# Products of probabilities and values in plain float32 in the two attention loops of a fused 4-layer block

## What is computed

```python
# stick-breaking, 16 heads of 64, query blocks of 128, keys before the query only
z = einsum('bhqd,bhkd->bhqk', q, k) * scale
log_stay = where(strict, log_sigmoid(-z), 0)
w = where(strict, exp(log_sigmoid(z) + reverse_cumsum(log_stay) - log_stay), 0)
out = einsum('bhqk,bhkd->bhqd', w, v)          # <- this product

# dilated: three banded softmax branches, merged by their denominators
p = exp(z - m);  den = sum(p)
o = einsum('brhnqk,brhnkd->brhnqd', p, v) / den   # <- and this one
```

## Time and profile before

| what | value |
|---|---|
| median of 3 runs | 2716.75 us |
| profiled execution, its own time | 2715.01 us |
| span of that execution in the trace | 2713.2 us |
| mean granted TensorE clock | 0.974 |
| TensorE matmul busy | 2593.8 us (96%) |
| VectorE / ScalarE / GpSimd busy | 1474.8 / 903.2 / 217.5 us |
| stick stage: fill and loop / drain | about 40 to 285 us / 285 to 317 us |
| dilated stage: fill and loop / drain | about 741 to 982 us / 982 to 1011 us |

### The profile page before, as it was taken

The page is one execution under the profiler, slowest core; times in us unless marked ns, Lnnn a source line. Parts: engine busy times, 40 slices in busy tenths (PEclk is TensorE's granted clock), DMA queues, the critical chain, the costliest instruction groups (busy, mean ns, idle before and its releaser), DMA issues.

```text
span 2713.2 us, 33021 instructions
## 1 busy us (share of the span) xinstructions
PE 2593.8 (96%) x12138; PEld 2125.8 (78%) x12138; DVE 1474.8 (54%) x2276; ACT 903.2 (33%) x1291; POOL 217.5 (8%) x201
## 2 busy tenths in 40 slices
PE   5999899999899989999999999999999998999998
PEld 4877678888677767888887888778888787788886
DVE  4556464553456655555326555476653466766644
ACT  3334242222334434222223233253331454533311
POOL 0000000000011100000002000000003164000031
PEclk8999799999999979999999999999999999999999
DMA  3111033322211103332222111223322321233332
GB/s 122 52 48 39 31 109 96 97 85 90 88 55 46 54 23 104 100 99 86 90 95 94 62 50 58 86 86 100 93 85 93 132 63 63 86 101 93 92 102 86
DMA packets 60918, 219.49 MB, mean 81 GB/s; under 512 B 6789, under 2 KB 7077, under 8 KB 60720
## 3 DMA queue, kind: packets, MB, share of 16 engines
q1 hardware_dynamic: 58752, 209.53, 24.6%
q0 software_dynamic: 2064, 8.97, 1.0%
q10 hardware_dynamic: 32, 0.02, 0.0%
HBM read 216.38 MB, written 2.12 MB: 81 GB/s over the span
## 4 chain that ended last, share of the span: by engine, by line
PE 84%; DVE 7%; ACT 4%; issue 3%; POOL 1%; DMA 0%; SPq 0%; DVEq 0%; ACTq 0%; POOLq 0%
PE ps L255 27%; PE ps L257 26%; PE ps L256 26%; PE ps L1683 2%; POOL dilated_t L1183 1%; ACT wh L241 1%; DVE wl L249 1%; PE ps L911 1%; DVE stick_left L1060 1%; PE ps L924 1%; ACT window_p L1350 1%; DVE rstd L441 0%; ACT dilated_pB L1002 0%; DVE dilated_pB L1077 0%; PE ps L1707 0%
## 5 line engine op out<-in xcount | busy, mean ns | idle before, releaser
L255 PE MATMUL ps<-xh,wh 128*128 128x512 f32 x2000 | 802.4, 401 | 15.6 <-DVE stick_qs L1172 5.7
L257 PE MATMUL ps<-xh,wl 128*128 128x512 f32 x2000 | 786.0, 393 | 0.0
L256 PE MATMUL ps<-xl,wh 128*128 128x512 f32 x2000 | 785.5, 393 | 0.0
L249 DVE TENSOR_TENSOR wl<-raw,wh 128x1024 fp32r<-128x1024 f32 x332 | 409.6, 1235 | 221.9 <-ACT wh L241 221.6
L241 ACT ACTIVATE wh<-raw 128x1024 fp32r<-128x1024 f32 x332 | 349.1, 1054 | 521.5 <-PE ps L257 504.9
L255 PEld LDWEIGHTS ps<-xh,wh 128*128 128x128 f32 x2000 | 380.8, 190 | 97.3 <-DVE wl L249 8.4
L257 PEld LDWEIGHTS ps<-xh,wl 128*128 128x128 f32 x2000 | 379.5, 190 | 81.8
L256 PEld LDWEIGHTS ps<-xl,wh 128*128 128x128 f32 x2000 | 380.9, 190 | 75.3 <-issue 0.5
L255 PE MATMUL ps<-wh,up_ah 128*128 128x512 f32 x528 | 209.5, 397 | 0.0
L257 PE MATMUL ps<-wh,up_al 128*128 128x512 f32 x528 | 209.3, 396 | 0.0
L256 PE MATMUL ps<-wl,up_ah 128*128 128x512 f32 x528 | 209.3, 396 | 0.0
(11 more groups left out here) (302 smaller groups left out, 3650.5 us busy)
## 6 DMA issues: line engine op xcount, KB each, us to landing
raw<-weights SPq DMA_DIRECT2D x388, 512.0 KB, 3.5
cst<-rows_d POOLq DMA_DIRECT2D x9, 512.0 KB, 5.1
hT<-x_t SPq DMA_DIRECT2D x8, 256.0 KB, 5.8
hgrn_mask<-levels POOLq DMA_DIRECT2D x1, 2048.0 KB, 8.2
window_bias<-bias_rows POOLq DMA_DIRECT2D x1, 2048.0 KB, 10.4
out_t<-hT SPq DMA_DIRECT2D x8, 256.0 KB, 2.2
cst<-consts SPq DMA_DIRECT2D x1, 960.0 KB, 7.9
stick_resets<-resets SPq DMA_DIRECT2D x1, 640.0 KB, 9.6
```

Of the source, the lines that this page charges most:

```text
L249: dve.tensor_tensor(wl[slot][:, :], raw[slot][:, :], wh[slot][:, :].bitcast(F32), ALU.subtract).then_inc(lo_done, 1)
L255: pe.matmul(out, w_hi, m_hi, start=first, stop=False, **kw)
L256: pe.matmul(out, w_hi, m_lo, start=False, stop=False, **kw)
L257: return pe.matmul(out, w_lo, m_hi, start=False, stop=last, **kw)
```

## The change

In both attention stages V and the transposed probabilities are kept as one plain float32 tensor each. `pe_values` issues one plain float32 matmul per block in place of three reduced ones. The low part of the probabilities (`dve_pT`, one VectorE instruction per head) and the low part of V (two per pair) are gone, with their signals; `pe_values` waits for ScalarE's copy alone, and the wait for V's tensor is for ScalarE's two copies. GpSimd clears one padded tensor of V per stage in place of two. What leaves is 16 `ptl` and 16 `vl` instructions per stage.

```diff
-                self.vh, self.vl = a("vh", [P, SB, 2, P], F32R), a("vl", [P, SB, 2, P], F32R)
+                self.v = a("v", [P, SB, 2, P])
-                self.pth, self.ptl = a("pth", [P, self.cols], F32R), a("ptl", [P, self.cols], F32R)
+                self.pt = a("pt", [P, self.cols])
...
         def pe_values(pe, a, j, hh):
-            pe.wait_ge(*a.pl_ready(2 * j + hh + 1))
+            pe.wait_ge(*a.pt_ready(2 * j + hh + 1))
             if hh == 0:
-                pe.wait_ge(*a.v_ready(j + 1))
+                pe.wait_ge(*a.v_ready(2 * j + 2))
             for kb in range(SB):
                 at, n = K_AT[kb], (SB - kb) * P
-                mm = products(pe, ps[:, 6, kb * P:kb * P + n], a.vh[:, kb, hh, :], a.vl[:, kb, hh, :],
-                              a.pth[:, at:at + n], a.ptl[:, at:at + n], hh == 0 and kb == 0,
-                              hh == 1 and kb == SB - 1, skip_group_check=True)
+                mm = pe.matmul(ps[:, 6, kb * P:kb * P + n], a.v[:, kb, hh, :], a.pt[:, at:at + n],
+                               start=hh == 0 and kb == 0, stop=hh == 1 and kb == SB - 1, skip_group_check=True)
             mm.then_inc(a.pv_done.sem, 1)
...
-            act.activation(a.pth[:, :], flat(3, 6)[:, 0:a.cols], ACT.Copy).then_inc(a.ph_ready.sem, 1)
+            act.activation(a.pt[:, :], flat(3, 6)[:, 0:a.cols], ACT.Copy).then_inc(a.pt_ready.sem, 1)
...
-                    act.activation(a.vh[:, :, v, v * HD:(v + 1) * HD], vT, ACT.Copy).then_inc(a.vh_ready.sem, 1)
+                    act.activation(a.v[:, :, v, v * HD:(v + 1) * HD], vT, ACT.Copy).then_inc(a.v_ready.sem, 1)
...
-        def dve_pT(dve, a, j, hh):
-            dve.wait_ge(*a.ph_ready(2 * j + hh + 1))
-            dve.tensor_tensor(a.ptl[:, :], flat(3, 6)[:, 0:a.cols], a.pth[:, :].bitcast(F32),
-                              ALU.subtract).then_inc(a.pl_ready.sem, 1)
...
             if attn:
-                dve_pT(dve, a, j, 0)
                 if a.kind == "stick":
                     dve_weights(dve, a, j, 1)
...
-            if attn:
-                dve_pT(dve, a, j, 1)
...
-            if proj:
-                dve.wait_ge(*a.vh_ready(2 * i + 2))
-                for v in range(2):
...
-                    m = dve.tensor_tensor(a.vl[:, :, v, cols], vT, a.vh[:, :, v, cols].bitcast(F32), ALU.subtract)
-                m.then_inc(a.v_ready.sem, 1)
```

More of the change, by code:

```diff
@@ L866, in __init__ @@
                 self.vs_ready, self.vT_done = Signal("pair_vs_ready", PAIRS), Signal("pair_vT_done", PAIRS)
-                self.vh_ready, self.v_ready = Signal("pair_vh_ready", HEADS), Signal("pair_v_ready", PAIRS)
+                self.v_ready = Signal("pair_v_ready", HEADS)
                 self.z_done, self.p_ready = Signal("pair_z_done", HEADS), Signal("pair_p_ready", HEADS)
-                self.pT_done, self.ph_ready = Signal("pair_pT_done", HEADS), Signal("pair_ph_ready", HEADS)
-                self.pl_ready, self.pv_done = Signal("pair_pl_ready", HEADS), Signal("pair_pv_done", HEADS)
+                self.pT_done, self.pt_ready = Signal("pair_pT_done", HEADS), Signal("pair_pt_ready", HEADS)
+                self.pv_done = Signal("pair_pv_done", HEADS)
                 self.oh_ready, self.o_ready = Signal("pair_oh_ready", PAIRS), Signal("pair_o_ready", PAIRS)
-                self.padded = Signal("pair_padded", 2)
+                self.padded = Signal("pair_padded", 1)
                 if kind == "stick":
@@ L947, in pe_pair @@
                 if attn:
-                    pe.wait_ge(*a.v_ready(i))
+                    pe.wait_ge(*a.v_ready(2 * i))
                 project(pe, ph, i, 0, ps[:, 7 if attn else 0, :], xh, xl, x_ready=x_ready)
@@ L1161, in dve_pair @@
                 dve.tensor_tensor(ol, src, oh.bitcast(F32), ALU.subtract).then_inc(a.o_ready.sem, 1)
-            if proj:
-                dve.wait_ge(*a.vh_ready(2 * i + 2))
-                for v in range(2):
-                    vT = ps[:, 7, :].rearrange("p (b d) -> p b d", b=SB)[:, :, v * HD:(v + 1) * HD]
-                    cols = slice(v * HD, (v + 1) * HD)
-                    m = dve.tensor_tensor(a.vl[:, :, v, cols], vT, a.vh[:, :, v, cols].bitcast(F32), ALU.subtract)
-                m.then_inc(a.v_ready.sem, 1)
         def take(dve, a, dst, bank=7):
@@ L2006, in _ @@
             pool.memset(stick.left[:, TRI:TRI + 1], 0.0).then_inc(ones_made, 1)
-            for v in (stick.vh, stick.vl):
-                pool.memset(v[:, :, :, :].bitcast(F32), 0.0).then_inc(stick.padded.sem, 1)
+            pool.memset(stick.v[:, :, :, :], 0.0).then_inc(stick.padded.sem, 1)
             pool.dma_start(table[0:BUCKETS, :], buckets).then_inc(sinks_in, 16)
             pool.dma_start(one_hot[0:BUCKETS + 1, :], onehot).then_inc(sinks_in, 16)
-            pool.wait_ge(*stick.padded(2))
+            pool.wait_ge(*stick.padded(1))
             pool.memset(table[BUCKETS:BUCKETS + 1, :], NEG).then_inc(sinks_neg, 1)
             pool.wait_ge(*o_up0.tile_done(KT))
-            for v in (dil.vh, dil.vl):
-                pool.memset(v[:, :, :, :].bitcast(F32), 0.0).then_inc(dil.padded.sem, 1)
+            pool.memset(dil.v[:, :, :, :], 0.0).then_inc(dil.padded.sem, 1)
             pool.wait_ge(loaded, 16 * 4)
@@ L2050, in attention_pe @@
                     stats=None if stats_bank is None else lambda: rms_pe(pe, r, stats_bank))
-            pe.wait_ge(*a.padded(2))
+            pe.wait_ge(*a.padded(1))
             with pe.Fori(1, PAIRS) as i:
```

## The result

The changed kernel takes 2686.03 us (median of 4 runs, 2679.3 to 2689.66) against 2716.74 for the kernel before, measured on the same chip. The ratio is 0.9887, with an interval of 0.9875 to 0.9898: 30.7 us less, where 8.7 were forecast. The profiled execution took 2689.66 with a span of 2687.9, against 2715.01 and 2713.2 before, so the traces have 25.3 us to account for. All times and medians here are of executions in the usual state of the chip; one of the four of the kernel `e3_three_no_low` took 4436.95 us at a mean granted clock of 0.66 and is left out.

The account below looks back on a forecast made before the run. TensorE, busy 96% of the span, was taken to bound the kernel. Stick loop +1.8, stick drain -3.5, dilated loop -3.7 and dilated drain -3.3 gave -8.7 us, from 2716.75 to 2708.0, range 2700.5 to 2716.5.

Parts of the forecast that it names:

- Part 1: Products with V: four plain ones take 2.17 us a head at full clock, +0.30; about 4.3 at half clock, +0.7.
- HGRN row: Profile row of HGRN's plain float32 product with V on 1280 columns, 2.20 us, used to price the new products.
- rival B: All 32 product groups: a plain group costs 1.30 times the reduced one, 2.43 us; total 2716.3; chance 0.12.
- Part 2: Stick loop: wait before the second head's turn goes, -4.8, second product +2.1; -2.7 us at unchanged clock.
- The clock: Stick loop: new iteration lengths shift the low-clock spells, from -12.5 to +6.7 us; +1.8 taken, leaning to more spells.
- rival A: Stick loop: the clock stays up, -25 us at most, about 2695; chance 0.10.
- Part 3: Stick drain: waits for the low part go; -1.2 us at low clock, -5.9 if the clock stays up; -3.5 taken.
- Part 4: Dilated loop: projection of v starts earlier, -0.83, second product +0.30; -0.53 us an iteration, -3.7 over seven.
- Part 5: Dilated drain: -1.3 us at low clock, -7 if turn, second product and output projection's start run at full; -3.3 taken.
- The sum: Whole kernel: +1.8 - 3.5 - 3.7 - 3.3 = -8.7 us, giving 2708.0.
- C: Both loops: low clock after every stretch of scores makes it slower, 2727.7 with one in each dilated iteration; chance 0.06.
- D: Both loops: the low part only covered other waits, so only the +0.30 a product remains; 2720; chance 0.06.

Follow-up runs that it names:

- e3_three_no_low: Kernel before with its three reduced products kept but the low part of the probabilities and its wait dropped, output wrong, for timing alone: 2682.28 us, ratio 0.9879.
- fourth kernel: Plain products as in the changed kernel, but VectorE still makes the low part of the probabilities and the product waits for it: 2724.19 us, ratio 1.0031.

## Why the prediction was wrong, point by point

**Part 1, the products: right.** 2.15 us at full clock (2.17 forecast) and 4.43 at half (about 4.3). The HGRN row was the right one to lean on; rival B, at 2.43, is out. By the Trainium skill (FP8 and Floating Point Precision, TensorE Precision Notes) true float32 takes four passes. By that, as an estimate, four times 1280 columns at 2.4 GHz are 2.13 us, and the trace agrees with its 2.15. To apply four against three to the old group (2.49) would have misled: its 1.87 are more than the 1.60 that the same working gives for three passes.

**Part 2, stick loop.** The lengths by kind were right: 30.79, 32.36 and 34.00 against 30.9, 32.4 and 34.1. The wait for the scan's product went, and TensorE is the later one, by 0.7 us (0.66 forecast). At an unchanged clock the forecast was -2.7; the second trace has 30.7 us of low clock in the loop, exactly as the kernel before, and gained 3.3.

**The clock is the step that failed.** In the stick loop the prediction took it for a loss: +1.8 where an unchanged clock gives -2.7, so +4.5 for the clock, on the ground that a spell had stood where the iteration was long. For the output projection with the dilated fill, and for what lies behind the dilated drain, it has no term and gives no reason. The runs showed a gain from the clock, in all three traces of the changed kernel, and not each time in the same places:

| stretch | forecast, us | first trace | second | third |
|---|---|---|---|---|
| start to first transposes | 0 | +1.1 | +1.0 | +0.8 |
| stick loop | +1.8 | -16.0 | -3.3 | -3.4 |
| stick drain | -3.5 | -3.7 | -6.5 | -6.5 |
| output projection to dilated fill | 0 | -4.7 | -5.2 | -5.2 |
| dilated loop | -3.7 | -2.65 | -4.2 | -4.2 |
| dilated drain | -3.3 | -3.8 | -4.9 | -4.9 |
| behind it, to the last matmul | 0 | +4.45 | -2.65 | -2.7 |
| sum | -8.7 | -25.3 | -25.8 | -26.1 |
| low clock (before: 130 us) | | 99 | 92 | 92 |

In the first trace the stick loop lost 27 us of low clock, the mechanism of rival A, with more than the -12.5 that I had for it. (That figure left the first iteration alone; it lost two of its three spells as well.) In the second and third the stick loop kept all of its 30.7 us, and 25 us went from the two drains, 10 from the projection and fill, 6 from behind the dilated drain. One number for the mix of a loop was the wrong kind of term.

**Part 3, stick drain: inside its bounds once, below them twice.** -3.7 in the first trace (-3.5 forecast). In the second and third traces it was -6.5, below the end of -5.9, since there the first product with V ran at full clock too (2.26 us in the second trace). The output projection's start at full clock (some 2 us) comes on top; I had counted it only in the low end. It is a part of the 4.7 us that projection and dilated fill lost with half of their 20.5 us of low clock, and the rest of that I had not priced.

**Part 4, dilated loop: right.** 30.01 us an iteration, 30.1 forecast; the waits of the projection of v are gone, save the one in the fill. The loop gave -4.2 in the second and third traces, without a spell (-3.7 forecast), and -2.65 in the first, which had one in its first iteration.

**Part 5, dilated drain: right in size.** -3.8 and -4.9 against -3.3, inside -1.3 to -7. The second product and the start of the projection were at full clock in all three traces, as the better end had it; the turn was so in the second (1.25 us) and in between in the first (1.93).

**The sum.** The terms at a fixed clock were -2.7 in the stick loop, -3.7 in the dilated one and some -2.5 in the drains at low clock, so about -9. That is about what is left when the low clock is taken off. A spell in the loop is 3.4 us of low clock and costs 1.60, so a microsecond of low clock costs up to 0.47 (less where TensorE waits anyway). In the three traces it fell by 31, 37 and 37 us, worth 14, 18 and 18, which leaves 11, 8 and 9 for the instructions. Over all executions it fell by some 47 us, worth 22 of the 26 to 31 us measured. The forecast had the instructions about right. For the clock it had +4.5 in the loop and some -4.3 in the drains, in sum about nothing, where it gave 14 to 22. The prediction said that this term spans 20 us, and still chose from its bad half. The evidence for that choice was a pattern in three kinds of iterations of one execution, and the second trace of the changed kernel shows that such a pattern need not hold even for the same instructions.

**The rivals.** A (2695) came nearest in time, still 9 us too high, but its mechanism, a clock that stays up in the stick loop, is that of the first trace alone; the second and third are as fast with nine spells there. It too left out the projection and fill, 4.7 to 5.2 us. C, low clock behind every stretch of scores, came true for single iterations of the second and third traces, beside drains with half the low clock of before. D (the low part was cover) is out for the changed kernel. The fourth kernel, where the wait ahead of the turn stays, shows about what it would have cost: 2724.19, against 2720 forecast for it.

**What stays open.** Why the low clock is less once VectorE no longer makes the low part. That it is less, the third and fourth kernels show. The plainest case is the changed kernel with nine spells in its loop: it has 10 and 10 us of low clock in its drains, while the kernel before, with nine, has 24 and 21. The gaps in the drains are shorter now (1.4 us ahead of the first stick product in place of 3.0, 1.3 ahead of the second dilated one in place of 2.9), which fits, but no run varied those gaps alone.

## What to carry to other kernels

Where TensorE is busy 96% of the time, look for what another engine does ahead of it: the low part was nobody's named wait in the loops, yet taking it away was the whole gain, and the slower plain products only cost a part of it. Price a change at a fixed clock first, and keep the clock as a separate term with both ends, for the whole span and not for one loop. Don't read its likely value from the pattern of one execution; take a second one, and compare the mean granted clocks of many. And when a piece of work is moved, ask what it covered: the scores that were dealt out had hidden `vl`.

## What the runs showed of the hardware that was not expected

- **The same program takes different low clock in each execution.** One trace of the changed kernel had one spell in the stick loop, the two others nine; the loops took 217.1, 229.8 and 229.7 us, the spans 2687.9, 2687.4 and 2687.0. What one stage loses another gives back, so the span moves much less than its parts. Stages of two single traces can't be compared by length without their granted clock beside them.
- **The low clock is no small matter in a kernel that keeps TensorE at 96%.** 130 us of low clock cost up to some 61 us of 2713, or 2.2%, in the kernel before (less where TensorE waits anyway). The Trainium skill (TensorE: Matmul & The Clock Gate, Part 1: The HAM clock gate) puts the cost of coming up to speed, as a kernel starts, at under 1% of a typical span. The low clock here lies for the most part in the middle of the kernel, of which that figure does not speak. That the count of slow matmuls at the start differs from run to run, as the same section says, holds in these traces for the falls in the middle.
- **Dense work doesn't keep the clock up by itself.** With PE busy equal to the length of the iteration, clock 0.90 and 1.00 both occur (34.00 and 30.79 us, same instructions). In the stick loops of eleven traces each of the 76 falls came within or just behind 3.6 us of scores on 64 rows; dealt out among projections of 128 rows, in pieces of at most 2.4 us, the same scores had none in 21 iterations. The dilated scores, on 64 rows as well but 2.1 us long, had a fall in 4 of 98 iterations, each time the first of the loop. So 64 rows alone don't bring a fall. Whether they matter beside the length of the stretch, no run shows.
